# Another order of the seven products, of the operand sums and of the row loads where two kinds of feed-forward start their way back

## What is computed

```python
# the RWKV mixer's end (first layer), then its product with mix_w_out
y = ((y - mean) * lax.rsqrt(var + RWKV_GN_EPS)).reshape(B, L, C) * ln_w + ln_b
return ((y + bonus) * g).astype(z.dtype)
h = h + jnp.concatenate([y_a, y_b], axis=-1) @ mix_w_out[j]

# convolutional feed-forward: u = rmsnorm(h) @ w_up, a 3-tap convolution along the sequence,
# gelu(gate half) * value half -> hidden (256 x 2816), then h + hidden @ w_down

def swiglu(h, wg, wu, wd):
    return (jax.nn.silu(h @ wg) * (h @ wu)) @ wd
def half_ffn(h, g, shift, scale, gate, wg, wu, wd):
    return h + 0.5 * gate * swiglu(modulate(rms_norm(h, g), shift, scale), wg, wu, wd)

# the second model's modulation: 18 x 1024 rows of w_mod times silu(c), and silu(c_ctx)
ml = jnp.split(s_lat @ w_mod[l] + b_mod[l], N_MOD, axis=-1)
```

## Time and profile before

| | us |
|---|---|
| time, median of 3 runs | 2859.06 (2857.87 to 2859.93) |
| time of the profiled execution | 2857.05 |
| its span, first to last instruction | 2855.8 |
| TensorE matmul (PE) busy | 2804.2, 98% |
| weight loads (PEld) busy | 2345.7, 82% |
| VectorE (DVE) busy | 1675.2, 59% |
| ScalarE (ACT) busy | 736.8, 26% |
| chain that ended last, by engine | PE 91%, DVE 5%, ACT 2%, issue 2% |
| granted TensorE clock, mean | 0.999 |

### The profile page before, as it was taken

How to read it: one execution, slowest core, us unless ns; L and a number is a source line. 1 busy time by engine, 2 the same in 40 slices (tenths; PEclk the granted TensorE clock), 3 DMA queues, 4 the chain that set the end, 5 groups by cost and what they waited for, 6 DMA issues and landing times.

```text
span 2855.8 us, 43226 instructions
## 1 busy us (share of the span) xinstructions
PE 2804.2 (98%) x17582; PEld 2345.7 (82%) x17582; DVE 1675.2 (59%) x3211; ACT 736.8 (26%) x1852; POOL 80.1 (3%) x93
## 2 busy tenths in 40 slices
PE   9998999999999999999999999999999999999999
PEld 8777999777999888888445488888888888766999
DVE  4675788364887678752137277783466673235664
ACT  2453341252441311101236121110211110234220
POOL 0131000300000000000000000000000000000000
PEclk9999999999999999999999999999999999999999
DMA  7202556733548465423121055533445423232544
GB/s 247 71 3 76 174 176 201 197 122 123 177 148 251 155 199 192 150 64 104 57 81 60 30 171 183 182 120 81 155 155 162 151 72 109 87 81 89 163 136 117
DMA packets 351304, 376.27 MB, mean 132 GB/s; under 512 B 7331, under 2 KB 306740, under 8 KB 350340
## 3 DMA queue, kind: packets, MB, share of 16 engines
q1 hardware_dynamic: 325828, 285.68, 32.7%
q10 hardware_dynamic: 23072, 82.52, 8.3%
q0 software_dynamic: 2208, 5.31, 1.0%
HBM read 372.44 MB, written 1.05 MB: 131 GB/s over the span
## 4 chain that ended last, share of the span: by engine, by line
PE 91%; DVE 5%; ACT 2%; issue 2%; DMA 0%; ACTq 0%; SPq 0%; DVEq 0%
PE acc L135 79%; PE aux L135 11%; PE aux L3101 1%; DVE sb_big L1606 1%; DVE sb_work L1606 1%; DVE sb_work L1821 0%; DMA sb_work<-c_decay 0%; DVE sb_work L979 0%; PE aux L2510 0%; ACTq L1586 0%; ACT acc L1784 0%; DMA sb_x<-xT 0%; DVE sb_big L1358 0%; DVE sb_work L3340 0%; DVE sb_work L993 0%
## 5 line engine op out<-in xcount | busy, mean ns | idle before, releaser
L135 PE MATMUL acc<-sb_xn,weights 128*128 128x256 f32 (+2 forms) x3968 | 881.6, 375 | 9.7 <-ACT sb_xn L315 3.6
L135 PEld LDWEIGHTS acc<-sb_xn,weights 128*128 128x128 f32 x3968 | 668.7, 190 | 184.1 <-issue 109.5
L135 PE MATMUL acc<-sb_work 128*128 128x256 f32 (+1 forms) x1880 | 361.1, 346 | 0.0
L135 PE MATMUL acc<-sb_big,weights 128*128 128x256 f32 (+1 forms) x1904 | 339.6, 336 | 8.6 <-ACT acc L1773 5.2
L135 PEld LDWEIGHTS acc<-sb_work 128*128 128x128 f32 x1880 | 312.9, 191 | 33.5 <-issue 0.5
L135 PE MATMUL acc<-sb_work,weights 128*128 128x256 f32 (+2 forms) x1636 | 337.8, 354 | 1.4 <-DVE sb_work L1515 1.4
L135 PEld LDWEIGHTS acc<-sb_big,weights 128*128 128x128 f32 x1904 | 301.1, 191 | 41.2 <-ACT acc L1773 7.0
L135 PEld LDWEIGHTS acc<-sb_work,weights 128*128 128x128 f32 x1636 | 268.7, 191 | 47.4 <-issue 21.1
L135 PE MATMUL acc<-sb_xn,sb_work 128*128 128x256 f32 (+1 forms) x1200 | 231.7, 342 | 0.0
L135 PEld LDWEIGHTS acc<-sb_xn,sb_work 128*128 128x128 f32 x1200 | 196.8, 191 | 19.8
L1606 DVE SCALAR_TENSOR_TENSOR sb_work<-sb_work 128x1024 f32<-128x1024 f32 x128 | 156.4, 1222 | 2.8
(11 more groups left out here) (422 smaller groups left out, 3275.0 us busy)
## 6 DMA issues: line engine op xcount, KB each, us to landing
weights<-ffn_w_up SPq DMA_DIRECT2D x88, 1024.0 KB, 8.0
sb_work<-w_mod_rows ACTq DMA_DIRECT2D x134, 512.0 KB, 5.8
weights<-ffn_w_down SPq DMA_DIRECT2D x48, 1408.0 KB, 7.2
weights<-ffn_w_gate SPq DMA_DIRECT2D x44, 1024.0 KB, 5.4
weights<-ple_w_gate SPq DMA_DIRECT2D x4, 2048.0 KB, 8.6
weights<-na_w_qkv SPq DMA_DIRECT2D x8, 1024.0 KB, 7.9
weights<-w_in SPq DMA_DIRECT2D x4, 2048.0 KB, 8.2
weights<-mix_w_in SPq DMA_DIRECT2D x7, 1024.0 KB, 9.2
```

The lines of the kernel that those rows point to most:

```text
L135: return te.matmul(o, lhsT, rhs, start=start, stop=stop, skip_group_check=True)
```

## The change

`BACK_PRODUCTS` goes. In step 22 the half feed-forwards use 1, 5, 6, 2, 7, 3, 4, and the convolutional ones 1, 5, 2, 6, 7, 3, 4. In the half feed-forwards the weight sums s3 and s4 no longer stand ahead of the activation sums: DVE's order after the last hidden tile is t1, t2, s3, t3, s4, t4 (before: s3, s4, t1, t2, t3, t4). In the convolutional ones s1 moves up, ahead of the result of product 7 of the last tile; t1, which needs hidden tiles 0 to 10 only, is done ahead of the last taps, then s2; after the last hidden tile come t2, s3, t3, s4, t4 (before: t1, t2, t3, s3, s4, t4). The three row loads and the condition's load are issued one a tile in tiles 16 to 19, after the copy of bank b to c. In the mixer's last product, each of the four k tiles is waited for by itself.

```diff
@@ -1459,6 +1459,8 @@
 
         def project(n, half_):
             for k in range(4 * (1 - half_), 4 * (1 - half_) + 4):
+                if half_ and n == 0:
+                    te.wait_ge(ya_ready.sem, ya_ready_at(k))
                 c = 128 * (n % 4)
                 ins_ = mm(acc[n // 2][:, L * (n % 2):L * (n % 2) + L], w[n // 4](k, c, c + 128),
                           yb[:, k - 4, :] if k >= 4 else ya[:, k, :], k == 4 and n % 2 == 0, k == 3)
@@ -1480,7 +1482,6 @@
                     te.wait_ge(gn_sq.sem, gn_sq_at(ct))
                     gn_var.on(mm(aux[ct][:, L:2 * L], blk64[:], yc[:, ct, :]))
             project(n, 0)
-        te.wait_ge(ya_ready.sem, ya_ready_at(CT - 1))
         for n in range(8):
             ins_ = project(n, 1)
             if n % 2:
@@ -1549,8 +1550,8 @@
     st_u, st_v, st_c12 = signal("partial_product_copied"), signal("lower_right_set"), signal("upper_right_set")
     st_g1, st_g2, st_hid = signal("left_gate_set"), signal("right_gate_set"), signal("hidden_half_set")
     st_x = signal("x_half_added")
-    PRODUCTS, BACK_PRODUCTS = (1, 5, 6, 2, 7, 3, 4), (1, 2, 5, 6, 7, 3, 4)
-    order_of = lambda i: BACK_PRODUCTS if i == FT else PRODUCTS
+    PRODUCTS, CONV_BACK = (1, 5, 6, 2, 7, 3, 4), (1, 5, 2, 6, 7, 3, 4)
+    order_of = lambda i, up: PRODUCTS if up or i != FT else CONV_BACK
     SUM_FOR, TERM_FOR, UP_TERM_FOR = {5: 0, 6: 1, 7: 2, 3: 3}, {5: 0, 6: 1, 7: 2, 4: 3}, {5: 0, 6: 1, 4: 2, 7: 3}
     FH = FT // 2
     sum_up = [area(work, 3072 + 512 * n, 4, 128) for n in range(3)]
@@ -1585,8 +1586,11 @@
         n0 = 128 * (R.first + t)
         rows_in[t % m].on(ac.dma_start(R.tiles[t % m], ins["w_mod_rows"][n0:n0 + 128, :]))
 
+    def scalar_rows_condition(R):
+        cond_in.on(ac.dma_start(R.silu_cond.rearrange("p s k -> p (s k)"), ins["cond_rows"]))
+
     def scalar_rows_begin(R):
-        cond_in.on(ac.dma_start(R.silu_cond.rearrange("p s k -> p (s k)"), ins["cond_rows"]))
+        scalar_rows_condition(R)
         for t in range(len(R.tiles)):
             scalar_rows_load(R, t)
 
@@ -1630,7 +1634,7 @@
             for i in range(self.start, n):
                 if i == 0:
                     self.plain = st_p.reserve(4)
-                for q in order_of(i) if i else ():
+                for q in order_of(i, up) if i else ():
                     if (i < FT and q == 4 and i % 2) or (i >= FT and q in PRODUCTS[-2:]):
                         self.done[i, q] = (acc_full, next(ends))
                     else:
@@ -1710,7 +1714,7 @@
             kt = 4 if up else FH
             operands = {1: (a11, b11), 2: (a12, b21), 3: (s4, b22), 4: (a22, t4), 5: (s1, t1), 6: (s2, t2), 7: (s3, t3)}
             banks = {1: bank_a, 2: bank_a, 3: bank_b, 4: bank_c, 5: bank_d, 6: bank_b, 7: bank_c}
-            for q in order_of(i):
+            for q in order_of(i, F.up):
                 if q in SUM_FOR:
                     te.wait_ge(st_s.sem, F.s(4 * j + SUM_FOR[q]))
                 if q in TERM_FOR and i in (F.base, FT):
@@ -1820,19 +1824,24 @@
                                   (a21, a11, a21, ALU.subtract), (s4, a12, s2, ALU.subtract))[n]
             st_s.on(ve.tensor_tensor(to, one, other, op))
 
+    def vector_first_term(F, i):
+        b11, b12 = F.activations(i)[0:2]
+        st_t.on(ve.tensor_tensor((F.sum_x if i < FT else F.sum_h)[0], b12, b11, ALU.subtract))
+
     def vector_activation_sums(F, i):
         b11, b12, b21, b22 = F.activations(i)
         t1, t2, t4 = F.sum_x if i < FT else F.sum_h
-        st_t.on(ve.tensor_tensor(t1, b12, b11, ALU.subtract))
+        if F.up:
+            vector_first_term(F, i)
         ve.wait_ge(st_t.sem, st_t.n)
         st_t.on(ve.tensor_tensor(t2, b22, t1, ALU.subtract))
         if i < FT:
             ve.wait_ge(st_t.sem, st_t.n)
             st_t.on(ve.tensor_tensor(t4, b21, t2, ALU.subtract))
             return
+        vector_weight_sums(F, FT, (2,))
         st_t.on(ve.tensor_tensor(b12, b22, b12, ALU.subtract))
-        if not F.up:
-            vector_weight_sums(F, FT, (2, 3))
+        vector_weight_sums(F, FT, (3,))
         ve.wait_ge(st_t.sem, st_t.n)
         st_t.on(ve.tensor_tensor(t4, b21, t2, ALU.subtract))
 
@@ -1935,8 +1944,8 @@
                 ve.wait_ge(F.done[i, 4][0].sem, F.done[i, 4][1])
                 ve.wait_ge(st_g1.sem, F.g1(i))
                 st_hid.on(ve.tensor_tensor(F.hv[:, i, 0:F.H], g1, bank_c[:, 0:F.H], ALU.mult))
-                if i >= FT - 2:
-                    vector_weight_sums(F, FT, (0, 1) if i == FT - 2 else (2, 3))
+                if i == FT - 2:
+                    vector_weight_sums(F, FT, (0, 1))
                 if F.rows and 1 <= i < ROWS_UNTIL:
                     for n in range(middle, F.rows.upto(i)):
                         vector_row(F.rows, n // 2, n % 2)
@@ -2092,6 +2101,10 @@
             scalar_conv_gelu(F, f - 1)
             ac.wait_ge(F.done[f, 6][0].sem, F.done[f, 6][1])
             st_u.on(ac.copy(c, b))
+            if FT - 6 <= f < FT - 6 + len(conv_tile):
+                scalar_rows_load(F.rows, f - FT + 6)
+            elif f == FT - 6 + len(conv_tile):
+                scalar_rows_condition(F.rows)
             ac.wait_ge(F.done[f, 2][0].sem, F.done[f, 2][1])
             if f >= 2:
                 ac.wait_ge(hid_set.sem, F.hid(f - 2))
@@ -2103,8 +2116,6 @@
             left_set.on(ac.copy(y[1][:, 0:128], c))
             ac.wait_ge(left_set.sem, left_set.n)
             scalar_conv_mid(F, f, 1)
-            if f == FT - 4:
-                scalar_rows_begin(F.rows)
         scalar_conv_gelu(F, FT - 1)
 
     def scalar_conv_ffn(F, following):
@@ -2173,6 +2184,8 @@
             vector_conv_sum(F, f + 1, 0)
             vector_conv_sum(F, f + 1, 1)
             vector_conv_hidden(F, f - 1)
+            if f == FT - 1:
+                vector_weight_sums(F.fast, FT, (0,))
             ve.wait_ge(st_u.sem, F.copied(f, 1))
             ve.wait_ge(F.done[f, 7][0].sem, F.done[f, 7][1])
             st_v.on(ve.tensor_tensor(y[1][:, 128:L], c, conv_d[:, f % 2, :], ALU.add))
@@ -2180,8 +2193,9 @@
             ve.wait_ge(F.done[f, 3][0].sem, F.done[f, 3][1])
             st_c12.on(ve.tensor_tensor(y[0][:, 128:L], b, conv_d[:, f % 2, :], ALU.add))
             vector_conv_sum(F, f + 1, 2)
-            if f == FT - 1:
-                vector_weight_sums(F.fast, FT, (0, 1))
+        ve.wait_ge(hid_set.sem, F.hid(FH - 1))
+        vector_first_term(F.fast, FT)
+        vector_weight_sums(F.fast, FT, (1,))
         for half in range(2):
             vector_conv_taps(F, FT - 1, half)
         vector_conv_hidden(F, FT - 1)
```

## The result

| | before | changed |
|---|---|---|
| median of 4 runs, us | 2858.47 (2857.18 to 2859.93) | 2843.53 (2842.43 to 2846.01) |
| profiled execution / its span, us | 2857.05 / 2855.8 | 2843.27 / 2842.0 |

The ratio is 0.9947 [0.9935, 0.996]: faster by 14.9 us where I had said 13.7. Between the two profiled executions the span fell by 13.8.

A forecast was written before the change was run, and what follows sets the result against it. TensorE, busy nearly throughout, was taken to bound the kernel. Gains of 4.44 + 1.3 + 4.1 + 2.85 + 1.0 = 13.7 us, taken from a median of 2859.06, gave 2845.4 us, range 2844.0 to 2850.0.

The forecast's parts named there:

- What bounds the kernel: Whole kernel: TensorE is busy nearly throughout and carries nine tenths of the chain, so only its earlier starts count.
- starts or idle column: TensorE's waits: measured by starts of weight loads they sum to 13.7 us, by the profiler's idle column 10.5; starts are right.
- Half: Step 22 of three 256-column half feed-forwards: both waits for ACT's copies vanish, 1.48 us each, 4.44 together.
- last half: Step 22 of the last, 128-column half feed-forward: both waits vanish, gain 1.3 us, with a margin of 0.16.
- convolutional: Step 22 of two convolutional feed-forwards: product 2's wait vanishes, the one before 7 stays; 2.05 us each, 4.1 together.
- row loads: Way up of two convolutional feed-forwards: loads issued one a tile no longer lengthen a tile, 1.24 and 1.61, gain 2.85 us.
- mixer: Mixer's end: TensorE starts once DVE's first of four tiles is ready, gain 1.0 us.
- A: Row loads: single issues still hold ACT, so nothing of the 2.85 us is won; 2848.2 us, chance 0.10.
- B: Step 22: product 5 or 6 waits for t1 or t2 instead, about 1 us kept per feed-forward; 2851.5 us, chance 0.08.
- C: Later joins: gains are given back where a transfer or DVE's rows end last; about 2857 us, chance 0.09.
- D: Convolutional tile 21: s1 waits for a late weight block, stopping DVE and then TensorE; slower, 2865.6 us, chance 0.03.
- the low end: Bottom of the predicted range for the whole kernel's time, 2844.0 us, allowing some tenths of scatter of the median.

The follow-up runs named there:

- the order alone: The changed kernel with its new order of products, but DVE's sums in the order of before: 2871.1 us, ratio 1.0044.

## Why the prediction was right in its parts and missed the time

*What bounds the kernel; starts or idle column.* Right. Every part measured by itself came out as by starts (1.49 a half feed-forward against 0.99 from the idle column; 3.0 against 2.1 for the wait of products 6 and 7).

*Half, last half, convolutional, row loads, mixer.* Right in mechanism and size, in the table above to within 0.05 each. With 13.6 in all the sum of 13.7 was 0.1 too high. That the three half feed-forwards are alike was taken from a total over six waits of unequal length, which doesn't show it; the starts do, 1.49 each.

*Rivals.* A fell with the rows alone: all of its 2.85 but 0.02 came. B didn't happen: t1, t2 and the weight sums were in time everywhere, the 0.16 of the last half feed-forward too. C didn't: no later stage is longer but for the clock at 545. D didn't: s1 started at 431.35, with no wait for a block of weights. Its mechanism exists, though, with another cause: the order alone shows that a late t1 costs twice, as a wait of 4.3 us and as a product at half the clock.

*The step that failed* is the last one of the sum: "that execution was 2.0 below the median of the runs, 2859.06, from which I predict 2859.06 - 13.7 = 2845.4", and with it the low end, "some tenths of scatter of the median". What the runs showed in its place: the profiled execution lies 1.25 and not 2.0 below the kernel's median, and the median moves with the number of low stretches by more than tenths. The miss of 1.9 has three parts. First, 2859.06 was the median of three executions, and 84 give 2858.3: 0.8 of it. Second, the sum was 0.1 high, the other way. Third, 2858.3 - 13.6 = 2844.7 is still 1.2 above the 2843.5 that 14 executions give, and no start of the changed steps holds that.

For the third the runs point at the clock. Without their low stretch of 1.7 the two profiled spans would be 2854.1 and 2840.3. A time is its span plus 1.25, so the medians, 2858.3 and 2843.5, stand for spans of 2857.05 and 2842.25: 2.9 and 1.9 above. As an estimate that is nearly two low stretches in the median execution of the kernel before and about one in that of the changed kernel. It makes 1.0 of the 1.2; the other 0.2 is the shift at 228 us. Executions with no low stretch bear it out. At a mean clock of 1.000 the half feed-forwards alone took 2849.5 (median of six), the rows alone 2852.5 (of five), the convolutional ones alone 2851.4 (both of two); each with its own gain in starts added (5.7, 2.8, 4.1) gives 2855.2 to 2855.5 for a kernel before without a low stretch, 3 below its median.

The profiled execution of the kernel before held one where its median execution holds about two, so it was the better start for the sum: 2857.05 - 13.7 = 2843.35 would have missed by 0.2, though partly by luck, since the changed kernel's median holds about one as well.

Why the changed kernel has fewer stays open. Filling two idle gaps moved the kernel before in the same direction by 1.6. The removed waits of 2 us at step 22 are no likely cause: in all six profiles of kernels that still have them the granted clock is 1.00 there. And the four parts alone, whose differences in time sum to 19.1, say that such a count doesn't add up by parts.

## What to carry to other kernels

Take a gain from the starts of the same instructions, with a wait counted as what a stretch has above its number of products; the idle column was a third too low here. Before the sum is set against a median, count the stretches at a lower clock in the profile and price them, and let the range reach one of them (here 1.7 us) to either side: for this change of 0.5% with well-known waits it was the largest error. A new order of products pays only if the engine that makes their operands gets an order to match, and DMA issues on a busy engine cost nothing here one at a time and over a microsecond four in a row.

## What the runs showed of the hardware that was not expected

A long wait of TensorE cost more than its length: after 4.27 us the next product of 22 records took 4.85 in place of 2.62 us, at a granted clock of half, in both convolutional feed-forwards. After the 1.75 us of the kernel before, a product took 2.72.

Apart from those at the long waits of the kernel with the order alone, the low stretches of all 17 profiles lie at three places, each right behind gaps of TensorE that are far shorter: near 220 us (gaps of 0.9, 0.7 and 1.6; five profiles), near 546 (1.3 and 1.6; ten) and near 1575 to 1583 (1.1 and 1.0; five). The gaps are in every profile that leaves them open, the low clock is not; two profiles, half feed-forwards alone and row loads alone, have it nowhere. A short stretch cost 1.5 to 1.7 us at the last two places and 0.6 to 0.8 at the first, a long one near 550 2.7 to 3.0. None of the profiles taken says what decides between the two.

Four DMA issues in a row (0.33, 0.78, 0.49 and 0.62 us on ACT's queue in the second convolutional feed-forward of the kernel before, 2.2 together) made a tile of TensorE 1.2 to 1.6 us longer, at either place tried.
